# A fused mixer and expert layer on one core: transfers reordered, small products grouped, a semaphore and an output start moved

## The reference, cut to what matters

```python
mod_x = silu(c) @ w_mod + b_mod                  # six vectors: shift, scale, gate, twice
hx = rmsnorm(x, g_mix) * (1 + x_sc1) + x_sh1     # the context likewise
ux, uc = hx @ w_in, hc @ w_in[:, 512:]
# left half of ux: means over windows of 2, 4, 8, 16, minus ux, times w_pool and s_pool
# right half: complex diagonal scans, forward and backward, 32 groups of 16 channels, 64 states;
# the latent scans start from the context's end states
y = Re(C_f h_f) + Re(C_b h_b) + ssm_d * u
y = gelu(y); ssm_x = y * sigmoid(y @ w_glu + b_glu)
x = x + x_g1 * (concat([pool_x, ssm_x]) @ w_out)
h2 = rmsnorm(x, g_ffn) * (1 + x_sc2) + x_sh2
eidx, gate = route(h2)                           # best group of 8 experts, then its best two
x = x + x_g2 * sum over the two experts e of gate_e * (silu(h2 @ w_gate[e]) * (h2 @ w_up[e])) @ w_down[e]
return rmsnorm(x, g_final)
```

## Time and profile before

| | |
|---|---|
| time, median of 3 runs | 651.88 us (651.62 to 654.46) |
| profiled execution | 656.37 us, of which the span is 654.2 us |
| busy share of the span | PE 90%, PE's weight loads 38%, DVE 30%, ACT 20%, POOL 8% |
| bytes moved | 249.02 MB, mean 381 GB/s |
| mean granted clock of PE | 0.967 of full speed |

### The profile page before, as it was taken

One profiled execution on the slowest core, in us unless ns is written; L12 is line 12 of the kernel. 1 busy time (PEld: TensorE's weight loads), 2 busy tenths in 40 slices (PEclk: granted clock), 3 DMA queues, 4 the chain that ended last, 5 costly groups with the idle time before them and its releaser, 6 DMA issues.

```text
span 654.2 us, 9323 instructions
## 1 busy us (share of the span) xinstructions
PE 589.0 (90%) x3774; PEld 248.9 (38%) x3774; DVE 196.4 (30%) x427; ACT 133.6 (20%) x229; POOL 51.6 (8%) x101
## 2 busy tenths in 40 slices
PE   1999997999979997999999799978988997899986
PEld 0454544464543342234334223423332342334332
DVE  7998499958730010002002000100100020011003
ACT  8661332040113111012111110202020111102112
POOL 3894000010020000000000000000000000000000
PEclk9999999998889999899999899989997998999999
DMA  8993799998879999999999999999999999998992
GB/s 311 422 399 132 264 328 343 411 410 367 311 260 406 423 420 422 422 418 373 418 421 422 423 421 422 423 421 422 422 421 422 423 421 421 422 421 319 407 413 80
DMA packets 43609, 249.02 MB, mean 381 GB/s; under 512 B 4776, under 2 KB 7480, under 8 KB 17216
## 3 DMA queue, kind: packets, MB, share of 16 engines
q1 hardware_dynamic: 40808, 243.93, 92.0%
q10 hardware_dynamic: 2424, 3.68, 1.7%
q0 software_dynamic: 352, 1.07, 0.5%
HBM read 244.46 MB, written 2.11 MB: 377 GB/s over the span
## 4 chain that ended last, share of the span: by engine, by line
PE 54%; DMA 22%; DVE 2%; issue 1%; SPq 1%; ACT 0%; DVEq 0%; ACTq 0%
PE ps L885 23%; PE ps L925 17%; DMA wts<-in_w_up 16%; PE ps L858 5%; PE ps L864 4%; DMA rc<-in_w_down 3%; DMA wts<-in_w_mod 2%; PE ps L821 2%; PE ps L901 1%; PE ps L792 1%; SPq L246 1%; PE ps L886 0%; DVE cb L1435 0%; DVE ra L1616 0%; PE ps L770 0%
## 5 line engine op out<-in xcount | busy, mean ns | idle before, releaser
L885 PE MATMUL ps<-wts,ra 128*64 128x512 f32 x512 | 240.8, 623 | 32.0 <-DMA wts<-in_w_up 29.2
L886 PE MATMUL ps<-wts,ra 128*64 128x512 f32 x512 | 240.9, 623 | 0.0
L885 PEld LDWEIGHTS ps<-wts,ra 128*64 128x64 f32 x512 | 69.7, 143 | 176.3 <-issue 135.6
L925 PE MATMUL ps<-wts,ra 128*32 128x512 f32 x512 | 111.4, 593 | 1.7 <-DMA rc<-in_w_down 1.7
L925 PE MATMUL ps<-rc,ra 128*32 128x512 f32 x512 | 111.4, 593 | 0.0
L1231 DVE TENSOR_TENSOR ra<-ra,ps 128x256 f32<-128x256 f32 x32 | 13.5, 422 | 263.1 <-ACT ra L1173 263.0
L1167 ACT COPY ra<-ps 128x512 f32<-128x512 f32 x32 | 33.6, 1050 | 213.0 <-PE ps L886 213.0
L886 PEld LDWEIGHTS ps<-wts,ra 128*64 128x64 f32 x512 | 69.7, 143 | 0.0
L925 PEld LDWEIGHTS ps<-wts,ra 128*32 128x32 f32 x512 | 29.9, 110 | 74.1 <-issue 73.5
L1231 DVE TENSOR_TENSOR cb<-ps,ra 128x512 f32<-128x512 f32 x32 | 22.1, 691 | 105.2 <-PE ps L925 105.2
L1162 ACT COPY ra<-ps 128x512 f32<-128x512 f32 x32 | 18.7, 585 | 145.7 <-PE ps L858 145.7
(11 more groups left out here) (234 smaller groups left out, 512.6 us busy)
## 6 DMA issues: line engine op xcount, KB each, us to landing
wts<-in_w_up SPq DMA_DIRECT2D x64, 1024.0 KB, 16.5
wts<-in_w_gate SPq DMA_DIRECT2D x64, 1024.0 KB, 13.8
wts<-in_w_down SPq DMA_DIRECT2D x30, 1024.0 KB, 15.8
rc<-in_w_down SPq DMA_DIRECT2D x30, 1024.0 KB, 19.7
wts<-in_w_mod SPq DMA_DIRECT2D x16, 1024.0 KB, 16.1
r<-in_w_mod SPq DMA_DIRECT2D x6, 1024.0 KB, 15.5
wts<-in_w_out SPq DMA_DIRECT2D x2, 2048.0 KB, 19.8
wts<-in_w_in SPq DMA_DIRECT2D x2, 1024.0 KB, 19.6
```

The costliest lines, as they stand in the source:

```text
L885: pe.matmul(ps[0:64, 4 + b, :], st, Wg[b][:, k, :], start=(k == 0), stop=(k == KD - 1))
L886: mm = pe.matmul(ps[64:128, 4 + b, :], st, Wu[b][:, k, :], start=(k == 0), stop=(k == KD - 1))
L925: mm = pe.matmul(ps[32 * j:32 * j + 32, BANKS[n], :], hid[:, j, f, SLOTS * t:SLOTS * t + SLOTS], Wd[j][:, f, 512 * h:512 * h + 512], start ...
```

## The change

- SP: the load of the SSM half of `w_out` goes behind the last piece of the scale. The four gate pieces and the load of `x` go ahead of the second half of the first up matrix and of three halves of down matrices. The first half of the second expert's up matrix is loaded after `glu_mm`, when the weights of the GLU in whose place it goes are used, no longer with the rest of that expert. Half a down matrix waits for `xa_ready` and no longer for `outs_started`.
- PE: the 128 end-state products stand in a row. The pool half for outputs 2 and 3 follows in groups: two products, the transposes, two products, and four behind the GLU. The last two of the four output starts stand behind the gate product, the last of them behind the counts. In every pass `scatter(0)` stands ahead of the fourth `gate_up`.
- DVE: the count of four for `out_copy` is given right after `gate_mm`.

```diff
-            sp.wait_ge(S("u_ssm_mm"), 4)
-            sp.dma_start(wo_ssm, w_out_v[:, 4:8, :]).then_inc(S("wo_ssm_in"), 16)
             sp.wait_ge(S("mod_used"), 14)
             last_third(0, 0)
...
             last_third(3, 0)
+            sp.wait_ge(S("u_ssm_mm"), 4)
+            sp.dma_start(wo_ssm, w_out_v[:, 4:8, :]).then_inc(S("wo_ssm_in"), 16)
             sp.wait_ge(S("mod1_row"), 16)
...
             gu_load(sp, 0, 0, 0, "up")
+
+            for j in range(4):
+                sp.wait_ge(S("mod2_used"), 2 * j + 2)
+                last_third(j, 1)
+            sp.wait_ge(S("y_mm"), 1)
+            for t in range(NT):
+                sp.dma_start(x2[:, t, :], x[0, t * P:(t + 1) * P]).then_inc(S(f"xres_in{t}"), 16)
             gu_load(sp, 0, 0, 1, "up")
-
             sp.wait_ge(S("hp_ready"), 1)
             for half in range(2):
                 down_load(sp, lambda j: j, half, (1,))
-            for j in range(4):
-                sp.wait_ge(S("mod2_used"), 2 * j + 2)
-                last_third(j, 1)
-                if j == 2:
-                    sp.wait_ge(S("y_mm"), 1)
-                    for t in range(NT):
-                        sp.dma_start(x2[:, t, :], x[0, t * P:(t + 1) * P]).then_inc(S(f"xres_in{t}"), 16)
             down_load(sp, lambda j: j, 0, (3,))
+            sp.wait_ge(S("glu_mm"), 2)
+            gu_load(sp, 1, 1, 0, "up")
             sp.wait_ge(S("mix_pool"), 1)
...
             sp.wait_ge(S("mix_mm"), 4)
-            gu_load(sp, 1, 1, 0)
+            gu_load(sp, 1, 1, 0, "gate")
             gu_load(sp, 1, 1, 1)
 
+            sp.wait_ge(S("xa_ready"), 3)
+            down_load(sp, lambda j: j, 0, (2,))
             sp.wait_ge(S("outs_started"), 1)
-            down_load(sp, lambda j: j, 0, (2,))
             sp.wait_ge(S("ss2_ready"), NT)
...
-                if m < 3:
-                    mix_pool(2, (m,))
             mm.then_inc(S("y_mm"), 1)
-            mix_pool(2, (3,))
-            mix_pool(3, (0,))
+            mix_pool(2, (0, 1))
...
             mm.then_inc(S("y_t"), 1)
-            mix_pool(3, (1,))
+            mix_pool(2, (2, 3))
...
-            mix_pool(3, (2, 3)).then_inc(S("mix_pool"), 1)
+            mix_pool(3).then_inc(S("mix_pool"), 1)
...
-            start_outputs(0)
-
-            start_outputs(1)
+            start_output(0)
+            start_output(1)
             gate_product().then_inc(S("gate_mm"), 1)
+            start_output(2)
 
             pe.wait_ge(S("score"), 1)
...
+
+            start_output(3).then_inc(S("outs_started"), 1)
...
                 turn_hidden(i, 1)
-                gate_up(i, 3)
                 pe.wait_ge(S("out_copy"), 4 * i + 4)
                 pe.wait_ge(S("pt_copy"), i + 1)
                 scatter(0)
+                gate_up(i, 3)
                 turn_hidden(i, 2)
...
             dve.wait_ge(S("gate_mm"), 1)
+            dve.sem_inc(S("out_copy"), 4)
             tt(Pm, iota4, columns(posx, slice(0, 4)), ALU.is_equal).then_inc(S("slots"), 1)
...
-            dve.sem_inc(S("out_copy"), 4)
             dve.wait_ge(S("g2_ready"), 1)
```

More of the change, by code:

```diff
@@ L785, in _, with start_output @@
                         mm.then_inc(S("glu_mm"), 1)
-            mix_pool(3, (2, 3)).then_inc(S("mix_pool"), 1)
-            def start_outputs(t):
+            mix_pool(3).then_inc(S("mix_pool"), 1)
+            def start_output(n):
+                t = n // 2
                 pe.wait_ge(S("x2_ready"), t + 1)
-                for n in (2 * t, 2 * t + 1):
-                    mm = pe.matmul(ps[:, n, :], ident, x2[:, t, 512 * (n % 2):512 * (n % 2) + 512], start=True, stop=False,
-                                   skip_group_check=True)
-                if t == NT - 1:
-                    mm.then_inc(S("outs_started"), 1)
+                return pe.matmul(ps[:, n, :], ident, x2[:, t, 512 * (n % 2):512 * (n % 2) + 512], start=True, stop=False,
+                                 skip_group_check=True)
             def turn_rows(t, half):
```

## The result

The changed kernel takes **648.05 us** (median of 13 executions, 646.58 to 655.41), the kernel before 653.42 us beside it (13 executions, 650.80 to 656.32): a ratio of **0.9933, 95% interval 0.9908 to 0.9959**. That is 4.4 us less; the forecast was 8.3 us less (643.6 us, range 640.5 to 647.5). A second timing gave 0.9951 (0.9918 to 0.9984). (A ratio leaves out executions that lie more than 1.5% above the fastest of their kernel; this took away four of the 25, and the mean of all 25 is 650.7 us.)

What follows compares the result with a forecast made beforehand. The loop was taken as paced by transfers, with time to win only where they idle. Gains of 1.3 + 0.9 + 2.8 + 1.7 + 1.6 = 8.3 us off 651.88 gave 643.6 us, range 640.5 to 647.5.

Steps and rivals of the forecast that it cites:

- T1: End of the first expert's first half on PE, 191.12 us before; bringing it forward moves the whole loop; forecast 184.4.
- Part 1, the gate piece: Transfers before the projection: the first gate piece lands 7.5 us earlier, at 133.0 us, so DVE stops waiting for it.
- Part 1, "their room is full before T1 either way": Expert loads before the loop: the early up half and earlier down half by themselves win nothing.
- Part 2, `y_mm` at 128.2: End states on PE finish about 2.8 us sooner, at 128.2 instead of 131; SSM half then starts 1.3 us earlier.
- The rival of the small products: End states: each of four groups stalls 1.14 us, `y_mm` at 131.6; that, or a clock fall, gives 644.9 to 645.3; chance 0.14.
- Part 2, the clock: SSM half: full clock worth 1.8 us, but a new wait for POOL may lower it; taken as 0, bounds 0 to 1.8.
- the first rival: The clock does not fall at the GLU, 1.8 us more gain, 641.8 us; chance 0.14.
- Part 3, output starts: Before the counts on PE: one output start leaves the path, gain 0.9 us, up to 1.3.
- Part 4, the count: Between first gather and first expert: early `out_copy` removes PE's wait, 2.8 us, and its slow clock, 1.7 us.
- the rival of another wait in the place of the semaphore: After the first gather: something else is ready only near 185.8 us, so 2.8 and 1.7 fall away; 648.9 us; chance 0.13.
- Part 5, the loop: Every pass: `scatter(0)` ahead of the fourth `gate_up` starts `down` sooner; gain 1.6 us in all, bounds 0 and 2.4.
- its two places: Stretches from 300 and 588 us, where transfers wait for PE, idle 2.0 and 3.4 us; 0.8 us gain at each.

Runs made afterwards that it cites:

- the base: Changed kernel with pool products back between the end states and all four output starts back ahead of the gate product; 644.14 us, ratio 0.9856 (0.9869 over four timings).
- the run with rows early and the broadcast late: The base with DVE's second rows ahead of the tests for further passes and POOL's `g_final` broadcast held until the last down pieces landed; 645.41 us, ratio 0.9889.
- the second trace: Changed kernel profiled again, nothing altered; T1 at 183.25 us, span 646.1 us; its timing gave a median of 652.80 us, ratio 0.9951.
- with full rows: Changed kernel with the gate's two one-row bias products replaced by products of all 128 rows, same order, number and columns; 647.86 us, ratio 0.9918.

## Why the prediction was wrong, and where it was right

- **What bounds the kernel: right.** In the twenty traces T1 lies between 179.7 and 191.7 us, and what follows it takes 459.2 to 463.1. An execution's time is read off T1 within 2 us; gains below that cannot be.
- **Part 1, the gate piece: right.** It landed at 133.2 us (forecast 133.0), and DVE waits for no load there; it waits for the transposes. In the timeline of DVE in the changed kernel:

```profile
135.56 1.66 DVE L1445 SCALAR_TENSOR_TENSOR rc<-ut,vt,ps 128x256 f32<-128x256 f32 x4 [3.13 <-PE ps L752]
```

- **Part 1, "their room is full before T1 either way": wrong.** I counted idle time of the transfers and not which load could use it. In the base the last down half hangs on DVE and comes 2.4 us ahead of T1 instead of 7.0, so the loop's first load lands 1.7 us later behind T1, as the run with rows early and the broadcast late shows.
- **Part 2, `y_mm` at 128.2: wrong**, it came at 128.14 + 3.63 = 131.8, no earlier than before. The rival of the small products had the right time (131.6) from the wrong cause: not four stalls of 1.14 us but one of 4.03, which ends behind an instruction packet, and 58 products at half clock behind it. I had counted the time that the pool products take and not that they stood in a stall. So its 1.3 us of earlier SSM half became -0.3 and 0.0 in the two traces. The Trainium skill, TensorE: Matmul & The Clock Gate, section Back-to-back issue gap, gives 81 ns a product, from which the estimate was 10.4 us for the 128 products; they took 9.9 us (121.90 to 131.77), so the sum was near, but not the pace: 70 products took 2.21 us, 32 ns each, and 4.03 us were the stall. By that estimate the time would have been 645.4 us (646.2, if the GLU moves with `y_mm` as in the rival of the stalls); the 648.05 measured say nothing for it, since they come in good part from the output starts.
- **Part 2, the clock: wrong in the safe direction.** PE did not wait for POOL ahead of the scale product, since the stall and the low clock brought it there only at 137.1 us; the clock did not fall at the GLU but earlier, behind the stall (0.50 from 128 to 132 us), and was back by 134 us; the SSM half took 3.60 us, 1.77 less. This is the first rival's 1.8 us. The terms together, 1.3 + 0, measured 1.5 to 1.8.
- **Part 3, output starts: this step failed most.** Its 0.9 us is 0 at full clock: the counts start 7.29 us behind the first output start instead of 7.73 with all four ahead, because PE then waits for DVE's chosen experts, and what is left of it is lost in the 0.47 us of issue ahead of the gather. And I bounded the clock by the 1.3 us that a start had taken at a partly low one, and never asked what stands between it and the next work of full rows: with two starts behind the gate product PE ran from 168 to 184 us at half clock. Against the second trace the same stretch took 15.59 instead of 9.30 us, 6.3 more. With a third to a half of the executions so, that is 2 to 3 us in the mean, which fits the means of all executions (650.7 us, and 647.6 with full rows): the larger part of what is missing from 8.3 us.
- **Part 4, the count: right on PE, mis-sized at the end.** 2.8 + 1.7 = 4.5 us was PE's loss in the one profiled execution; in another it was 2.9, and 1.6 to 2.2 of it are given back at the last down half and the broadcast. Measured at the end 0.2 to 1.3. The remainder, between that and the 1 to 2.7 of the traces, is within what these timings can tell, and stays open. So does the rival of another wait in the place of the semaphore: it came true, in the queue of the transfers, not on PE.
- **Part 5, the loop: right by the times**, 2.1 to 2.9 us for 1.6 from six executions each; neither of its two places is shown. The 302 GB/s from 588 us, on which the second rested, are 378 in the second trace of the kernel before.
- **The sum.** The parts that I priced low (transfers 1.3, measured 3.6 to 4.8) and those that I priced high (starts, count) would nearly have met: the base, without the two parts of PE's order, has the 8.6 us.

## What to carry to other kernels

Price a wait that goes by what then stands next in the queue of transfers, too: list the last loads ahead of the point that you move, and the engine for which each of them waits. Work placed in a stall whose end it does not move is free, and collecting it elsewhere makes it cost. Where the clock may be low, keep products of all rows ahead of products of one row, as the base does; and look at a second trace of the kernel before, as a loss of clock seen in one execution need not belong to the others.

## What the runs showed of the hardware

- A DMA queue named "instruction" moved packets of 0.02 MB; here two of them lay 6.0 to 6.2 us apart while the transfers' engines were full, and PE's stalls ended 2.2 to 2.8 us behind them. From the first end state on PE stopped after 140 records and after 128 more, in every trace that has these stalls. 70 products of 64 rows and 128 columns took 2.21 us; that PE uses up its instructions faster than they come is inferred.
- Behind a stall of 4.03 us PE ran at a granted clock of 0.50 (1.2 GHz), behind one of 2.26 us at the same place at 1.00.
- PE, busy without a gap from 168 to 184 us, stayed at a granted clock of 0.50 with products of one row among its work; with 128 rows in their place no execution took as long as those, and none of 11 had a mean clock below 0.965, against 9 of 25.
- POOL's broadcast of 512 KB took 3.6 us from issue to landing where nothing else was loaded (issued 629.27, held back to the end), and 5.6 to 7.5 us beside the last down half.
- The engines of the transfers counted as busy in the first microsecond of a load while little moved. In the base, where the last down half and the broadcast start out of an empty queue (last columns: DMA share, GB/s):

```profile
179.00:180.00 1.00, 1.00 (x6) 0.28 (x4) 0.00 (x0) 0.00 (x0) 0.00 (x0) 1.00 0.97 188
...
181.00:182.00 1.00, 1.00 (x11) 1.00 (x10) 0.00 (x0) 0.23 (x1) 0.00 (x0) 1.00 1.03 434
```

With the broadcast held back, the down half alone shows the same: a share of 0.38 at 74 GB/s in its first microsecond.
